# Convolution sums held in PSUM, Fourier tiles in other banks, four output weight blocks held at once, and head norms split by token parts

## The reference

```python
h  = rmsnorm(x, norm_mix_g[0])
p  = h @ w_in_ab                                   # 1024 -> 512 + 512 + 512
ya = fnet_heads(p[..., :512], fnet_map)            # 4 heads: 2-D FFT, real part, times a 128x128 map
u  = p[..., 512:1024] * sigmoid(p[..., 1024:])     # 4 heads of 128 channels
u  = depthwise_conv(u, conv_w, 31 taps) + conv_b   # along the 512 tokens
yb = silu(layernorm(u, per head of 128 channels) * g + b)
x  = x + concat([ya, yb]) @ w_out_ab               # 1024 -> 1024
h  = rmsnorm(x, norm_ffn_g[0])                     # and the first gated feed-forward follows
```

## Time and profile before

| | |
|---|---|
| median of 3 runs | 2945.78 us (2945.59 to 2949.7) |
| the profiled execution | 2939.21 us, its span 2937.2 us |
| PE busy | 2686.4 us, 91% of the span |
| PEld, DVE, ACT, POOL busy | 2156.1, 1327.5, 694.8, 1354.4 us |
| granted TensorE clock, mean | 0.959 |
| HBM read | 232.21 MB |

### The profile page before, as it was taken

One profiled execution on the slowest core, in us unless ns is written; L12 is line 12 of the kernel. 1 busy time (PEld: TensorE's weight loads), 2 busy tenths in 40 slices (PEclk: granted clock), 3 DMA queues, 4 the chain that ended last, 5 costly groups with the idle time before them and its releaser, 6 DMA issues.

```text
span 2937.2 us, 39587 instructions
## 1 busy us (share of the span) xinstructions
PE 2686.4 (91%) x14612; PEld 2156.1 (73%) x14612; DVE 1327.5 (45%) x1868; ACT 694.8 (24%) x1294; POOL 1354.4 (46%) x862
## 2 busy tenths in 40 slices
PE   7588999998999998889989999999778888999997
PEld 6366777776777777666868888888567767778886
DVE  7953222234222236444354444434756555345545
ACT  2022000022000013566131000000455455211112
POOL 7226555544555553133545343343433221486662
PEclk9799999999999999899989999999899999999998
DMA  5013444443444441000111111111001010223221
GB/s 188 24 50 118 146 145 143 143 137 118 147 145 143 143 136 58 29 1 1 44 43 58 64 57 57 62 59 57 29 29 43 29 43 15 71 88 99 93 93 57
DMA packets 67368, 235.55 MB, mean 80 GB/s; under 512 B 8144, under 2 KB 9552, under 8 KB 67152
## 3 DMA queue, kind: packets, MB, share of 16 engines
q1 hardware_dynamic: 65792, 233.64, 24.3%
q10 hardware_dynamic: 1488, 0.69, 0.1%
HBM read 232.21 MB, written 2.10 MB: 80 GB/s over the span
## 4 chain that ended last, share of the span: by engine, by line
PE 79%; DVE 8%; issue 6%; ACT 3%; POOL 3%; DMA 1%; DVEq 0%; SPq 0%; ACTq 0%; POOLq 0%
PE ps L529 63%; PE ps L972 2%; PE ps L944 2%; PE ps L669 2%; PE ps L871 1%; PE ps L857 1%; PE ps L994 1%; DVE X L1809 1%; PE ps L647 1%; DVE q L1856 1%; DMA raw<-in_stream 1%; PE ps L572 1%; PE ps L678 1%; ACT arena L1030 1%; PE ps L833 1%
## 5 line engine op out<-in xcount | busy, mean ns | idle before, releaser
L406 POOL TENSOR_SCALAR whi<-raw 128x1024 fp32r<-128x1024 f32 x334 | 374.0, 1120 | 1299.5 <-DMA raw<-in_stream 1299.4
L408 POOL TENSOR_TENSOR wlo<-raw,whi 128x1024 fp32r<-128x1024 f32 x334 | 825.5, 2472 | 27.9
L529 PE MATMUL ps<-Ahi,whi 128*128 128x512 f32 (+1 forms) x2192 | 758.6, 376 | 80.4 <-DVE tmp L1700 25.5
L529 PE MATMUL ps<-Alo,whi 128*128 128x512 f32 (+1 forms) x2192 | 751.9, 373 | 0.0
L529 PE MATMUL ps<-Ahi,wlo 128*128 128x512 f32 (+1 forms) x2192 | 750.2, 372 | 0.0
L529 PEld LDWEIGHTS ps<-Ahi,whi 128*128 128x128 f32 x2192 | 390.7, 192 | 181.2 <-issue 32.2
L529 PEld LDWEIGHTS ps<-Ahi,wlo 128*128 128x128 f32 x2192 | 390.9, 191 | 73.7
L529 PEld LDWEIGHTS ps<-Alo,whi 128*128 128x128 f32 x2192 | 390.7, 192 | 69.4
L529 PE MATMUL ps<-hhi,whi 128*128 128x512 f32 x1120 | 376.4, 373 | 16.8 <-DVE X L1809 15.7
L529 PE MATMUL ps<-hhi,wlo 128*128 128x512 f32 x1120 | 372.4, 370 | 0.0
L529 PE MATMUL ps<-hlo,whi 128*128 128x512 f32 x1120 | 372.1, 369 | 0.0
(11 more groups left out here) (249 smaller groups left out, 2810.4 us busy)
## 6 DMA issues: line engine op xcount, KB each, us to landing
raw<-in_stream SPq DMA_DIRECT2D x430, 512.0 KB, 3.7
X<-in_xT SPq DMA_DIRECT2D x2, 1024.0 KB, 6.6
arena<-in_dft SPq DMA_DIRECT2D x1, 2048.0 KB, 16.7
out_xT<-X SPq DMA_DIRECT2D x2, 1024.0 KB, 4.3
X<-in_ctxT SPq DMA_DIRECT2D x1, 1024.0 KB, 19.1
vec<-in_vec SPq DMA_DIRECT2D x1, 364.5 KB, 7.7
arena<-in_fmap SPq DMA_DIRECT2D x1, 256.0 KB, 12.2
arena<-in_cosq ACTq DMA_DIRECT2D x1, 256.0 KB, 2.7
```

The lines of the kernel that those rows point to most:

```text
L406: pool.tensor_scalar(whi[:, s, part], raw[:, s, part], 1.0, 1.0, ALU.mult, ALU.mult).then_inc(sem("w_hi"), 1)
L408: pool.tensor_tensor(wlo[:, s, part], raw[:, s, part], whi[:, s, part], ALU.subtract).then_inc(sem("w_split"), 1)
L529: mm = pe.matmul(dst[c], w[:, b % RING, off:off + P], rhs(k, part, c0, n), start=(k == 0 and w is whi and part == 0), stop=(k == kn - 1 an ...
```

## The change

1. **Taps.** The running sums of a pair lie in PSUM banks 2 and 3 (`CONV_BANK`). Each tap reads `upad` from SBUF and the sum from PSUM and writes PSUM; the last writes `conv` in SBUF. The loops are written out. The gates of tiles 2 and 3 come after tap 14 of the first pair (`GATES_AT`), no longer behind its last tap.
2. **Banks.** `win[5]` goes to banks 6 and 7, `pf` is copied from banks 0, 1, 6, 7, and the four Fourier results use banks 0 and 1 in turn.
3. **Norm of the heads.** Heads 0 and 1 are done among the taps of heads 2 and 3 (`LO_AT`, `NORM_AT`, `LAST_LO_AT`). The sums of squares are taken by quarters of the tokens: 32 partitions hold 128 tokens each, so root and reciprocal work on 128x128 in `std`, and four matmuls spread the inverse to 128x512 in PSUM.
4. **Four weight blocks.** Block 9 no longer goes through the ring but, after `y_done` 4, into the place of `dft`. Blocks 6 to 9 stay until the end; PE takes all tiles for the heads 0 to 3, then 4 and 5, then 6 and 7, with the norm's matmuls in between.

```diff
+WOUT_BANK = (6, 7, 4, 5, 0, 1, 2, 3)
+PF_BANK = (0, 1, 6, 7)
+CONV_BANK = 2
+GATES_AT = 14
+LO_AT = {14: 0, 18: 1, 22: 2, 26: 3}
+NORM_AT = {19: "centred", 23: "inverse", 26: "scaled"}
+LAST_LO_AT = 29
...
+        w9 = nc.alloc_sbuf_tensor_at("w9", [P, BLK], F32, offset=arena_at)
+        w9lo = nc.alloc_sbuf_tensor_at("w9lo", [P, BLK], F32R, offset=arena_at)
+        w9hi = nc.alloc_sbuf_tensor_at("w9hi", [P, BLK], F32R, offset=arena_at + 4 * BLK)
...
+        def norm_bank(h):
+
+            return 4 + h if h < 2 else h
...
+            last = B_WOUT + 3
+            for b in range(RING, last):
+                for half in range(2):
+                    sp.wait_ge(*when("w_used", 2 * (b - RING) + half + 1))
+                    load(b, b % RING, half)
+            sp.wait_ge(*when("y_done", HEADS_A))
+            for half in range(2):
+                part = slice(half * HALF, (half + 1) * HALF)
+                sp.wait_ge(*when("w_split", SPLITS[B_WOUT] + half + 1))
+                sp.dma_start(w9[:, part], ins["stream"][last, :, part]).then_inc(sem(f"raw{last % RING}{half}"), 16)
+            for b in range(last + 1, last + RING):
+                for half in range(2):
+                    sp.wait_ge(*when("w_used", 2 * (b - RING) + half + 1))
+                    load(b, b % RING, half)
...
-            split_run(0, B_FF[0])
+            split_run(0, B_WOUT + 3)
...
+                pool.tensor_scalar(w9hi[:, part], w9[:, part], 1.0, 1.0, ALU.mult, ALU.mult).then_inc(sem("w_hi"), 1)
+                pool.wait_ge(*when("w_hi", SPLITS[b] + half + 1))
+                pool.tensor_tensor(w9lo[:, part], w9[:, part], w9hi[:, part], ALU.subtract).then_inc(sem("w_split"), 1)
             band_matrices()
...
-            columns("win_done", win[5:6], X_ONLY, banks[2:4])
+            pe.wait_ge(*when("sig", 4))
+            columns("win_done", win[5:6], X_ONLY, banks[6:8])
...
+            def fourier(h):
                 pe.wait_ge(*when("z", h + 1))
...
+                if h >= 2:
+                    pe.wait_ge(*when("mix_out", h - 1))
...
+            def conv_means(heads):
+                for h in heads:
+                    pe.wait_ge(*when("conv", h + 1))
+                    pe.matmul(ps[:, norm_bank(h), :], ones[:, :], conv[:, h, :], start=True, stop=True).then_inc(sem("cmu"), 1)
+
+            def conv_squares(heads):
+                for h in heads:
+                    pe.wait_ge(*when("csq", h + 1))
+                    for q in range(4):
+                        mm = pe.matmul(ps[32 * q:32 * q + 32, norm_bank(h), 0:P], ones[:, 0:32], tmp[:, h, q * P:(q + 1) * P],
+                                       start=True, stop=True, skip_group_check=True)
+                    mm.then_inc(sem("cvar"), 1)
+
+            def conv_spread(heads):
+                for h in heads:
+                    pe.wait_ge(*when("crstd", h + 1))
+                    for q in range(4):
+                        mm = pe.matmul(ps[:, norm_bank(h), q * P:(q + 1) * P], ident[:, 32 * q:32 * q + 1].to_broadcast([P, P]),
+                                       conv_inv(h), start=True, stop=True, skip_group_check=True)
+                    mm.then_inc(sem("cspread"), 1)
+
+            def wout(tiles, first, end):
+
+                for j in tiles:
+                    b = B_WOUT + j // 2
+                    for k in range(first, end):
+                        pe.wait_ge(*when("mix_out", k + 1))
...
+                        hi, lo = (w9hi, w9lo) if j >= 6 else (whi[:, b % RING, :], wlo[:, b % RING, :])
+                        for w, a in ((hi, Ahi), (hi, Alo), (lo, Ahi)):
...
+                    if end == KT:
+                        mm.then_inc(sem("w_used" if j % 2 else "wout_done"), 2 if j % 2 else 1)
+
+            pe.wait_ge(*when("dft", 16))
+            fourier(0)
+            fourier(1)
+            pe.wait_ge(*when("z", 3))
+            conv_means((0, 1))
+            fourier(2)
+            conv_squares((0, 1))
+            fourier(3)
+            conv_spread((0, 1))
+            pe.wait_ge(*when("z", 4))
+            wout((0, 1), 0, 4)
+            pe.wait_ge(*when("cy", 2))
+            wout((2, 3), 0, 4)
+            conv_means((2, 3))
+            wout((0, 1, 2), 4, 6)
+            conv_squares((2, 3))
+            wout((3,), 4, 6)
+            wout((4,), 0, 6)
+            conv_spread((2, 3))
+            wout((5,), 0, 6)
+            pe.wait_ge(*when("cy", 4))
+            wout((6, 7), 0, 6)
+            wout(range(8), 6, KT)
...
             fourier_mid(0)
             fourier_mid(1)
...
+            fourier_mid(2)
+            fourier_out(0)
+            fourier_mid(3)
+            fourier_out(1)
+            conv_squared((0, 1))
             fourier_out(2)
+            conv_roots((0, 1))
             fourier_out(3)
...
+            conv_out((0, 1))
...
+            conv_squared((2, 3))
+            conv_roots((2, 3))
+            conv_out((2, 3))
...
+            def taps(pair, done, tap):
+
+                for n, t in enumerate(pair):
...
+                    sums = ps[:, CONV_BANK + n, :]
...
+                    dve.wait_ge(*when("tap", done + n - 1))
+                    last = tap == TAPS - 1
+                    dve.scalar_tensor_tensor(out=conv[:, t, :] if last else sums, in0=shifted, scalar=vec[:, at:at + 1], in1=sums,
+                                             op0=ALU.mult, op1=ALU.add).then_inc(sem("conv" if last else "tap"), 1)
...
+            for tap in range(TAPS):
+                taps((0, 1), 2 * tap, tap)
+                if tap == GATES_AT:
+                    gated(2)
+                    gated(3)
+            for tap in range(TAPS):
+                taps((2, 3), 2 * (TAPS - 1) + 2 * tap, tap)
+                if tap in LO_AT:
+                    h = LO_AT[tap]
+                    split_lo("mix_out", "mix_hi", h, ps[:, h % 2, :], T)
+                if tap in NORM_AT:
+                    for h in range(2):
+                        steps[NORM_AT[tap]](h)
+                if tap == LAST_LO_AT:
+                    for h in range(2):
+                        split_lo("mix_out", "mix_hi", 4 + h, tmp[:, h, 0:T], T)
```

More of the change, by code:

```diff
@@ L380, in _ @@
             sp.dma_start(X[:, :, T:TT], ins["ctxT"]).then_inc(sem("tables"), 16)
-            with sp.Fori(1, N_BLOCKS // RING) as i:
+            last = B_WOUT + 3
[12 more added lines that the diff above has]
+                    load(b, b % RING, half)
+            assert (last + RING) % RING == 0
+            with sp.Fori((last + RING) // RING, N_BLOCKS // RING) as i:
                 for s in range(RING):
@@ L487, in band_matrices @@
                                        ALU.add).then_inc(sem("bands"), 1)
-            split_run(0, B_FF[0])
+            split_run(0, B_WOUT + 3)
+            for half in range(2):
+                b = B_WOUT + 3
+                part = slice(half * HALF, (half + 1) * HALF)
+                pool.wait_ge(*when(f"raw{b % RING}{half}", 16 * (b // RING) + 16))
+                pool.tensor_scalar(w9hi[:, part], w9[:, part], 1.0, 1.0, ALU.mult, ALU.mult).then_inc(sem("w_hi"), 1)
+                pool.wait_ge(*when("w_hi", SPLITS[b] + half + 1))
+                pool.tensor_tensor(w9lo[:, part], w9[:, part], w9hi[:, part], ALU.subtract).then_inc(sem("w_split"), 1)
             band_matrices()
@@ L1122, in fourier_out, with conv_squared, conv_roots @@
                 act.wait_ge(*when("y_done", h + 1))
-                copy(Ahi[:, h, 0:T], ps[:, h, :]).then_inc(sem("mix_hi"), 1)
+                copy(Ahi[:, h, 0:T], ps[:, h % 2, :]).then_inc(sem("mix_hi"), 1)
+            def conv_squared(heads):
+                for h in heads:
+                    act.wait_ge(*when("cd", h + 1))
+                    act.activation(tmp[:, h, 0:T], conv[:, h, :], ACT.Square).then_inc(sem("csq"), 1)
+            def conv_roots(heads):
+                for h in heads:
+                    act.wait_ge(*when("cvar", h + 1))
+                    act.activation(conv_root(h), ps[:, norm_bank(h), 0:P], ACT.Sqrt, scale=1.0 / P,
+                                   bias=epsr[:, 1:2]).then_inc(sem("cstd"), 1)
@@ L1125, in _, with conv_out @@
+            def conv_out(heads):
+                for h in heads:
+                    act.wait_ge(*when("cy", h + 1))
+                    act.activation(tmp[:, h, 0:T], conv[:, h, :], ACT.Silu, bias=v("conv_ln_b", h)).then_inc(sem("csilu"), 1)
+                for h in heads:
+                    act.wait_ge(*when("csilu", h + 1))
+                    copy(Ahi[:, 4 + h, 0:T], tmp[:, h, 0:T]).then_inc(sem("mix_hi"), 1)
             fourier_mid(0)
             fourier_mid(1)
-            for h in range(2, HEADS_A):
-                fourier_mid(h)
-                fourier_out(h - 2)
+            fourier_mid(2)
@@ L1530, in _ @@
+            for step in (centred, inverse, scaled_conv):
+                for h in range(2, 4):
+                    step(h)
+            for h in range(2, 4):
```

(1 more changed line is left out.)

112 lines of the change are left out of this document (44 added, 68 removed).

## The result

| | before | after |
|---|---|---|
| median of 4 runs | 2946.21 us (2945.59 to 2949.7) | 2899.66 us (2896.36 to 2906.09) |
| ratio to before, 95% interval | | 0.9844 (0.9825 to 0.9862) |
| the profiled execution, its span | 2939.21, 2937.2 us | 2902.76, 2900.9 us |

The forecast was 2894.9 us. The change is worth 46.5 us of the 50.9 forecast. Two further sets of runs of the same kernel gave ratios of 0.9838 and 0.9826, so 0.983 to 0.984 is the fair figure; the forecast as a ratio is 0.9827. Each of these ratios has an interval of 4 to 7 us to either side.

A forecast was written before the change was run, and what follows sets the result against it. PE is busy 91% of the span, so time lies only where PE waits. PE's full work at 193.4 instead of 244.26 gains 50.9 us: 2945.78 - 50.9 = 2894.9 us; range 2887 to 2912 (8 in 10).

The forecast's parts named there:

- PE's chain: PE's work from the end of block 5 at 87.10 to the output product's end at 177.5: sum 90.4 us.
- the wait for ACT's copies: PE, before `z`, waits for the third of ACT's six copies: 1.6 us.
- The tap: DVE's tap with its sum in PSUM takes a pitch of 0.665 us, the row of L1433's shape.
- rival of two cycles per element: Taps reading and writing one PSUM bank take two cycles per element, pitch 1.2 us: 2959 us, chance 0.05.
- the slowness beside POOL: First-pair taps stay slow while POOL splits weights and take 70.6 us again: 2924 us, chance 0.05.
- The rule on access overhead: The skill's PSUM overhead on 124 taps would take 8 us more, some 6 reaching the end: 2901 us.
- DVE's margins: DVE's taps and norm pieces come 1.5 to 2 us before PE asks; a pitch up to 0.68 costs nothing.
- The one disturbance forecast: POOL's split of block 9 may hold up low parts of heads 4 and 5: 140 instead of 137.6; PE asks at 140.3.
- The margin at the squares: ACT squares one tile by 117.9; PE asks after the third Fourier head at 119.7: margin 1.8 us.
- The rival in which the pieces wait for each other: One late norm piece among the taps stops those behind it: 14 us more, 2909 us, chance 0.06.
- Behind the product: Block 12 loads from 177.5, lands in 3.7 us; POOL's three halves take 12.2; PE at full work at 193.4.
- Block 13: Its slot is free about 7.5 us behind the product, at 185.0; it lands at 188.7, before its turn at 189.2.

The follow-up runs named there:

- SBUF experiment: The changed kernel with the running sums of the taps back in SBUF (the tile conv) instead of PSUM, everything else as changed: 2929.33 us, ratio 0.9939.
- longer taps: The changed kernel with a small extra DVE instruction, a memset of 128x64 float32, behind every tap: 2900.83 us, ratio 0.9853.
- the norm behind the taps: The changed kernel with the norm of heads 0 and 1 moved from among the taps to behind them on all engines, four blocks kept: 2906.7 us, ratio 0.9879.
- gates late: The changed kernel with the last gates computed ahead of tap 30 instead of tap 14: 2894.66 us, ratio 0.9834.
- early blocks: The changed kernel with blocks 10 and 11 loaded before the product's end, blocks 12 to 14 taking ring slots: 2893.12 us, ratio 0.9802; again 2891.21 us, 0.9826.
- ring kernel: The changed kernel with output weights through the ring of three, so the product starts behind the norm of all four heads: 2922.67 us, ratio 0.9907.
- taps only: The changed kernel with the norm of all heads behind the taps and output weights through the ring of three: 2916.84 us, ratio 0.9911.

## Why the prediction was right, step by step

- *PE's chain.* Forecast 90.4 us from the end of block 5 to the end of the product, measured 179.34 - 88.67 = 90.7, and 177.92 - 87.24 = 90.7 in the repeated run. All its terms hold: the wait for ACT's copies (forecast 1.6, is 1.7), `z` (6.9, is 7.0), the Fourier heads, means and squares (from 99.22 to 129.17, 29.95 for a sum of 29.9).
- *The tap.* Forecast 0.665 us, is 0.66, and 750 ns for one where L1433 had 733 to 748. The rival of two cycles per element is out. So is the slowness beside POOL in PSUM; the SBUF experiment shows that it would have cost 32 us: the rival had reckoned 2924, the experiment gave 2929. The two first taps of a pair take 1.43 us of the row (46.58 to 48.01) instead of the 1.33 reckoned, which nothing waits for.
- *The rule on access overhead.* The Trainium skill ("Perfetto Trace Analysis", section "Optimizing Scalar/DVE Operations") has PSUM at about 125 ns against 60 ns for SBUF, from which the prediction worked out an estimate of 2901 us. No run shows the difference on back-to-back instructions: a tap with its sum in SBUF and one with it in PSUM both have a place of 0.66 us when POOL is idle.
- *DVE's margins.* The four low parts, the norm of heads 0 and 1 and the last taps all came in time; PE waits for none. The one disturbance forecast, low parts beside the split of block 9, came with 3.08 us for two and was covered. The margin at the squares was underestimated: 1.8 us, about 3 by the run with longer taps.
- *The rival in which the pieces wait for each other* did not occur. Its price was reckoned at 14 us; with the norm really behind the taps the loss is 8.5 us up to the means of heads 2 and 3.
- *Behind the product: the term that was mis-sized.* I reckoned 15.9 us from the product's end to full work (193.4 - 177.5). It took 18.3, 17.1 and 17.0 in three executions. I gave block 12 the median landing of 3.7 us. But blocks 10, 11 and 12 are asked for at 174, 176.7 and 179.6, 2 x 512 KB each, and the windows of the DMA in after say what they meet (length, clock, DMA share, GB/s):

```profile
176.00:178.00 2.00, 1.00 0.98 322
178.00:180.00 2.00, 1.00 0.99 340
180.00:182.00 2.00, 1.00 1.07 303
```

  The DMA engines are full, and block 12 stands behind block 11, which is still on its way (block 10 has just landed): 5.86 us in the chain shown above. In the two repeated runs the same half lands in 5.1 and 4.3 us. Blocks that used to come one by one, as `wout` gave slots back, now come all at once, because all four output blocks are held to the end. With them loaded before, block 12 stands behind no other, and the gap is 11.0 us; that version also frees block 13 from the wait of the next point, so it doesn't price the two apart.
- *Block 13.* I had its slot free 7.5 us behind the product. It was 8.7 (188.10 - 179.34), since the first use of the adaptive weights ran at half clock, which the last section shows. In both repeated runs that, and not block 12, was the last wait: POOL waited 0.20 and 1.02 us for block 13 before its third half.
- The remaining 1.6 us of the first profile's delay are its start (88.67 for 87.10), which the repeated runs (87.22 and 87.24) don't have.

Cut by parts, by ratios times 2945.8: taps in PSUM with the new banks and smaller norm steps 26 us; the four blocks, with the norm behind the taps, another 9.5; the norm among the taps 10 to 16 more. The four blocks pay without the norm among the taps, but not the other way round: without the fourth block the pieces among the taps gain nothing. The traces confirm the order of these (214.99, 203.10, 195 to 198 for PE's full work). Each ratio has an interval of 4 to 9 us to either side, so the middle part, 9.5 us, is shown by the traces and not by the times.

## What to carry to other kernels

When one engine is slow only while another works on the same memory, move the operand that can move, and judge the price from a row of the same shape with that operand elsewhere. Follow the gain until the next engine runs full: what is late next is priced from there, and a transfer that now starts together with others does not land in its median time. Splitting a dependent chain into pieces among other work pays only when someone waits for the pieces early; so test such parts both together and apart.

## What the runs showed of the hardware that was not expected

- *The clock behind the product.* Windows of PE in after over the norm `n2` and the adaptive product (length, busy, clock, DMA):

```profile
171.50:179.34 7.84, 7.84 (x35) 1.00 0.55 180
179.34:181.40 2.06, 1.81 (x49) 1.00 0.99 314
181.40:184.80 3.40, 0.98 (x23) 0.85 0.91 289
184.80:190.50 5.70, 5.69 (x41) 0.50 0.24 78
```

  PE had worked at 2.4 GHz without a wait since 92 us, then waited 0.2 and 2.2 us, and ran on at 1.2 GHz. The same small matmuls took 2.08 and 3.64 us, against 1.16 and 1.93 before behind the same two waits, where the granted clock stayed at 1.00 and only the 35 us of the product lay between these waits and those of the norm. So 2.6 us were lost behind this wait. The spread of the inverse, the first of these two, took 2.0 to 2.1 us in the repeated runs and with gates late, longer taps or early blocks too, 1.70 in the ring kernel, 1.40 with taps only, and 1.16 with the norm behind the taps and with taps in SBUF. Why the clock falls in one case and not in the other is not settled.
- *A `tensor_scalar` that writes PSUM.* 804 to 808 ns for 128x512 in the changed kernel, 532 to 541 ns with SBUF in and out (the experiment with taps in SBUF). The Trainium skill says that a PSUM operand costs an fp32 instruction its doubled mode: "VectorE: DVE Perf Modes", section "Why PSUM operands drop a tier"; these rows agree in direction.
- *Small instructions between large ones.* A memset of 128x64 takes 112 ns by its record, but puts only 0.045 us on the row of taps.
